# Expert products of a mixture layer: all 1024 gate columns first, then the up columns, instead of two half-width passes over both

## What is computed

```python
gu = rows @ w_gate_up[e] + b_gate_up[e]          # 1024 -> 2048
gate = jnp.minimum(gu[:, :D_FF], SWIGLU_LIMIT)   # D_FF = 1024, limit 7
up = jnp.clip(gu[:, D_FF:], -SWIGLU_LIMIT, SWIGLU_LIMIT)
hid = (up + 1.0) * (gate * jax.nn.sigmoid(gate * SWIGLU_ALPHA))
return hid @ w_down[e] + b_down[e]               # 1024 -> 1024
```

## Time and profile before

| | us |
|---|---|
| median of 3 runs | 2472.63 (2472.3 to 2474.09) |
| the profiled execution, its own time | 2471.6 |
| its span, first to last instruction | 2469.9 |
| PE busy | 2341.7 |
| DVE busy | 1807.0 |
| ACT busy | 1402.9 |
| granted TensorE clock, mean | 0.979 of full speed |

### The profile page before, as it was taken

How to read it: one execution, slowest core, us unless ns; L and a number is a source line. 1 busy time by engine, 2 the same in 40 slices (tenths; PEclk the granted TensorE clock), 3 DMA queues, 4 the chain that set the end, 5 groups by cost and what they waited for, 6 DMA issues and landing times.

```text
span 2469.9 us, 39207 instructions
## 1 busy us (share of the span) xinstructions
PE 2341.7 (95%) x11242; PEld 1577.9 (64%) x11243; DVE 1807.0 (73%) x2101; ACT 1402.9 (57%) x1441; POOL 257.3 (10%) x252
## 2 busy tenths in 40 slices
PE   6999999999948999999999999999999999999898
PEld 3454445545536777677777777777776777776443
DVE  4582555544557889788989988898877787897374
ACT  2112354434435777667777777677766676776344
POOL 1200000001230000100000001000111010010230
PEclk9999999999959999999999999999999999999999
DMA  6006910052238999999999999899988898997761
GB/s 198 22 13 216 355 36 22 14 185 77 69 96 287 333 352 354 336 311 362 345 375 351 360 365 348 307 338 375 351 287 312 278 360 292 367 347 260 267 221 51
DMA packets 291338, 629.50 MB, mean 255 GB/s; under 512 B 21633, under 2 KB 69505, under 8 KB 291218
## 3 DMA queue, kind: packets, MB, share of 16 engines
q1 hardware_dynamic: 235538, 532.20, 61.4%
q10 hardware_dynamic: 40304, 55.05, 6.2%
q0 software_dynamic: 15440, 41.51, 5.2%
HBM read 558.55 MB, written 68.57 MB: 254 GB/s over the span
## 4 chain that ended last, share of the span: by engine, by line
PE 75%; DVE 12%; issue 5%; DMA 5%; ACT 2%; DVEq 1%; SPq 1%; POOL 0%; ACTq 0%; POOLq 0%
PE bank L610 13%; PE bank L612 12%; PE bank L611 12%; PE bank L1368 6%; DVE wlo L876 6%; PE bank L780 4%; PE bank L1481 4%; PE bank L1391 3%; PE bank L671 3%; DMA raw<-in_w_down_dram 3%; PE bank L1358 2%; PE bank L1411 2%; PE bank L1440 2%; PE bank L1426 2%; PE bank L580 2%
## 5 line engine op out<-in xcount | busy, mean ns | idle before, releaser
L876 DVE TENSOR_TENSOR wlo<-raw,whi 128x2048 fp32r<-128x2048 f32 x456 | 1038.1, 2287 | 203.2 <-PE bank L612 159.8
L1753 ACT ACTIVATE whi<-raw 128x2048 fp32r<-128x2048 f32 x456 | 872.4, 1915 | 351.0 <-PE bank L612 172.8
L610 PE MATMUL bank<-whi,xhi 128*128 128x512 f32 x1216 | 498.3, 410 | 4.2 <-issue 4.2
L612 PE MATMUL bank<-wlo,xhi 128*128 128x512 f32 x1216 | 481.4, 396 | 0.0
L611 PE MATMUL bank<-whi,xlo 128*128 128x512 f32 x1216 | 481.0, 396 | 0.0
L610 PEld LDWEIGHTS bank<-whi,xhi 128*128 128x128 f32 x1216 | 228.7, 188 | 93.3 <-issue 43.4
L612 PEld LDWEIGHTS bank<-wlo,xhi 128*128 128x128 f32 x1216 | 228.8, 188 | 55.0
L611 PEld LDWEIGHTS bank<-whi,xlo 128*128 128x128 f32 x1216 | 229.1, 188 | 47.0
L610 PE MATMUL bank<-whi,hhi 128*128 128x512 f32 x608 | 246.0, 405 | 0.0
L612 PE MATMUL bank<-wlo,hhi 128*128 128x512 f32 x608 | 237.6, 391 | 0.0
L611 PE MATMUL bank<-whi,hlo 128*128 128x512 f32 x608 | 236.9, 390 | 0.0
(11 more groups left out here) (294 smaller groups left out, 2767.3 us busy)
## 6 DMA issues: line engine op xcount, KB each, us to landing
raw<-in_w_gate_up_dram SPq DMA_DIRECT2D x608, 512.0 KB, 6.5
raw<-in_w_down_dram SPq DMA_DIRECT2D x152, 1024.0 KB, 10.5
expert_rows<-zeros ACTq DMA_DIRECT2D x1, 33280.0 KB, 105.5
expert_rows<-ysb ACTq DMA_DIRECT2D x38, 512.0 KB, 8.1
xall<-in_x_dram SPq DMA_DIRECT2D x8, 512.0 KB, 11.0
uT<-in_w_out_dram SPq DMA_DIRECT2D x1, 4096.0 KB, 12.8
raw<-in_w_ple_gate_dram SPq DMA_DIRECT2D x1, 4096.0 KB, 19.8
h<-h_scratch SPq DMA_DIRECT2D x8, 512.0 KB, 6.2
```

The lines of the kernel that those rows point to most:

```text
L610: pe.matmul(dst, stat_hi[:, kt], hi, start=first, stop=False)
L612: return pe.matmul(dst, stat_hi[:, kt], lo, start=False, stop=last)
L876: dve.tensor_tensor(wlo[:, c % LO], raw[:, c % RAW], whi[:, c % HI].bitcast(F32), ALU.subtract).then_inc(lo_ready, 1)
L1753: act.activation(whi[:, c % HI], raw[:, c % RAW], ACT.Copy).then_inc(hi_ready, 1)
```

## The change

Pieces 0 to 3 now hold 256 rows of all 1024 gate columns, pieces 4 to 7 those of the up columns; each is one transfer with rows of 4 KB. Gate is limited once, 1024 wide, after piece 3; one sigmoid and one product of that width follow. On ACT the sigmoid stands behind hi of piece 9, as the first half's did. On DVE the product now stands before lo of piece 8. PE computes the first half (512 columns) of pieces 6 and 7, signals `up_done`, and then does their second halves; the first transposition of `hid` stands between these two. The next item's rows are transposed after piece 7 instead of after piece 8. DVE's lo of pieces 9, 10, 11 and 0', 1', 2' is moved one step later in its program. The tail has one chain of width 256 for gate and one for up: limit of gate after piece 3', transposes after piece 4.

```diff
-                half, p = c // 4, c % 4
-                rows = w_gate_up[0, bass.ds(e, 1), p * 256:p * 256 + 256, :].rearrange(
+                g, p = c // 4, c % 4
+                rows = w_gate_up[0, bass.ds(e, 1), p * 256:p * 256 + 256, g * DFF:g * DFF + DFF].rearrange(
                     "e (k p) n -> p (e k) n", p=P)
-                for g in range(2):
-                    sp.dma_start(parts[:, g], rows[:, :, g * DFF + half * 512:g * DFF + half * 512 + 512]
-                                 ).then_inc(raw_in[slot], 16)
+                sp.dma_start(dst.rearrange("p (k d) n -> p k (d n)", k=2), rows).then_inc(raw_in[slot], 16)
...
             def gate_piece(n, c, turns):
+                if c == 6:
+                    gate_part(n, 6, 0)
+                    pe.wait_ge(lo_ready, PIECES * n + 8)
+                    gate_part(n, 7, 0).then_inc(up_done, 1)
+                if c == 7:
+                    turns()
+                if c < 6:
+                    gate_part(n, c, 0)
+                return gate_part(n, c, 1)
...
+            def gate_clamp(n):
+                dve.wait_ge(w_free, PIECES * n + 4)
+                dve.wait_ge(hid_ready, 2 * n)
+                dve.wait_ge(gs_done, n)
+                dve.tensor_scalar(gat[:], banks(gate_base(0), 2), LIMIT, None, ALU.min).then_inc(gat_ready, 1)
+            def gate_product(n):
+                dve.wait_ge(sig_done, n + 1)
+                dve.tensor_tensor(sig[:], gat[:], sig[:], ALU.mult).then_inc(gs_done, 1)
+            def up_half(n, half):
+                if half == 0:
+                    dve.wait_ge(up_done, n + 1)
+                else:
+                    dve.wait_ge(w_free, PIECES * n + 8)
...
+                dve.tensor_scalar(upc[:], banks(gate_base(1) + half), LIMIT, -LIMIT, ALU.min, ALU.max).then_inc(gu_used, 1)
+                dve.wait_ge(gs_done, n + 1)
...
                 dve.scalar_tensor_tensor(out=hid[:], in0=upc[:], scalar=1.0, in1=sig[:, half * 512:half * 512 + 512], ...)
...
             def body(n, k1, tail):            # DVE
                 for c in range(PIECES):
+                    if c == 3:
+                        gate_clamp(n)
+                    if tail and c == 4:
+                        tail_up(k1)
+                        tail_gated(k1)
+                    if c == 4:
+                        gate_product(n)
                     if c == 5:
                         items.ahead(n + 1)
+                    if c in (6, 7):
+                        up_half(n, c - 6)
...
+                    if c < 5:
                         dve.wait_ge(w_free, PIECES * n + c + 1)
                         split_lo(n, c + LO)
+                    if c in (6, 7, 8):
+                        dve.wait_ge(w_free, PIECES * n + c)
+                        split_lo(n, c + LO - 1)
+                    if c == 6:
+                        hidden(n, 0)
+                    if c >= 9:
                         with dve.If(nxt > 0):
                             if c == 9:
                                 columns(n + 1)
+                            dve.wait_ge(w_free, PIECES * n + c)
+                            split_lo(n + 1, c + LO - PIECES - 1)
+                            if c == 11:
+                                dve.wait_ge(w_free, PIECES * n + PIECES)
+                                split_lo(n + 1, LO - 1)
...
             def body(n, k1, tail):            # PE
-                    if tail and c == 1:
-                        turn_tail_hidden(k1, 0)
+                    if tail and c == 4:
+                        turn_tail_hidden(k1)
-                    if c == 8:
+                    if c == 7:
...
                         with pe.If(nxt > 0):
                             turn_rows(n + 1)
...
             def body(n, k1, tail):            # ACT
+                    if tail and c == 5:
+                        tail_hidden(k1)
+                    elif c == 7:
...
+                            split_hi(n + 1, c + HI - PIECES)
+                            columns(n + 1)
...
                     if c == 3:
-                        sigmoid(n, 0)
+                        sigmoid(n)
```

More of the change, by code:

```diff
@@ L510, in raw_value @@
         def raw_value(n, c):
[L512 to L514 removed]
+            return 32 * n + 16 * (c // RAW + 1)
         class Items:
@@ new lines, in gate_part @@
+            def gate_part(n, c, half):
+                g, p = c // 4, c % 4
+                base = gate_base(g)
+                if p == 0 and half == 0:
+                    if g == 0:
+                        pe.wait_ge(xlo_ready, n + 1)
+                        pe.wait_ge(y_used[0], n)
+                    else:
+                        pe.wait_ge(gu_used, 2 * n)
+                if p == 0 and half == 1:
+                    if g == 0:
+                        pe.wait_ge(bias_in[0], 32 * n + 32)
+                        pe.wait_ge(y_used[1], n)
+                    mm = bias_pair(base, g, True)
+                    if g == 1:
+                        mm.then_inc(bias_used[0], 1)
+                for k in range(2):
+                    mm = three(banks(base + half), xhi, xlo, 2 * p + k, c, 2 * k + half,
+                               p == 0 and half == 0 and k == 0, p == 3 and k == 1)
+                return mm
@@ L682, in tail_piece, with turn_tail_hidden @@
                 mm.then_inc(tail_free, 1)
[L684 to L687, removed]
+            def turn_tail_hidden(k1):
+                hold(pe, hid_t_ready, k1 + 1)
+                hold(pe, ht_ready, k1)
+                for s in range(2):
+                    mm = pe.transpose(banks(XT)[:, s * P:s * P + P], hid_t[:, s * P:s * P + P], ident)
+                mm.then_inc(htt_done, 1)
             turn_rows(0)
@@ L976, in body @@
                                 columns(n + 1)
[L977 to L984, removed]
+                            dve.wait_ge(w_free, PIECES * n + c)
[3 more added lines that the diff above has]
+                                split_lo(n + 1, LO - 1)
                     if c == 11:
                         with dve.If(nxt2 > 0):
-                            tail_first(nk1, 0, items.kf + tail)
+                            tail_gate(nk1, items.kf + tail)
             items.run(body)
@@ L1821, in body @@
                         act.activation(mark[:], ident[:, 0:1], ACT.Sigmoid).then_inc(table_set, 1)
-                    if c == 7:
-                        sigmoid(n, 1)
-                    if tail and c == 5:
-                        tail_sigmoid(k1, 1)
                     if c in (6, 8):
                         hidden(n, c // 8)
-                    if tail and c == 6:
-                        tail_hidden(k1, 1)
+                    if c == 6:
+                        with act.If(nxt2 > 0):
+                            tail_columns(nk1)
                     if c == 11:
```

178 lines of the change are left out of this document (70 added, 108 removed).

## The result

The changed kernel takes 2510.42 us (median; 2508.51 to 2510.92, 4 runs) where the kernel before, on the same chip, takes 2472.47: a ratio of 1.0151, 95% interval 1.0139 to 1.0163. Forecast were 2504 us, so +32 against a measured +38. The direction and most of the size came out; the place did not. The forecast had over two thirds of the loss in plain items. Nearly all of it sits in the six items that stand before a tail, and in the tail items.

What follows compares the result with a forecast made beforehand. PE's 38.0 us per item and the nearly equal ring of raw slots were taken as the bound. Plain items +22.8, before tails +9, behind tails +1.5, tail items -1.6 made +32: 2504 us, own range 2484 to 2525, overall 2456 to 2535.

Steps and rivals of the forecast that it cites:

- The chain: DVE and ACT, plain item: first up limit follows hi of 9, sigmoid, product, lo of 8, register reads; 0.5 us late.
- register reads 1.08: DVE, plain item: register reads between lo of piece 8 and the first up limit take 1.08 us.
- U: Start of the first up limit on DVE: 1.5 us late in every plain item, with nothing hiding it.
- Piece 9 in plain items: Load of piece 9 lands 1.0 us later than today, between bounds of 0 and 2.5.
- The ring of slots: Raw slots for pieces 5' and 6' come free 3.1 and 3.6 us later, as DVE's lo's move back.
- PE alone: PE's own work in a plain item: changes sum to -0.32 us, so an item could take 37.7.
- Items before a tail: Six plain items before a tail: its traffic comes 4 us earlier and meets piece 9; net +1.5 us each.
- The upper bound of 2.5: Most by which piece 9 lands later: slots 3.1 us later, less 3 x 0.2 for shorter transfers.
- Tail items: Eight items with a tail: PE waits 0.4 us less in piece 1, 0.25 more in piece 7; -0.2 each.
- Items behind a tail: Five plain items after a tail: the longer tail item has filled the ring; +0.3 us each.
- the ring is not late: Rival: piece 9 lands at least 0.5 us sooner, plain items gain 0.3, kernel 2456 us; chance 0.22.
- 2 us less for a piece in one transfer: DMA estimate from the skill's page: standing alone, a piece costs 4.4 us in one transfer, 6.4 in two.

Runs made afterwards that it cites:

- ScalarE's order: Changed kernel with ScalarE applying the sigmoid before it makes the bf-rounded part of piece 9, not behind it: 2467.12 us, ratio 0.9987.
- VectorE's order: Changed kernel with VectorE making the lo of piece 8 before the gate's product, the sigmoid left in place: 2481.89 us, ratio 1.0046.
- the cured kernels: Changed kernel with sigmoid ahead of piece 9's rounding (2467.12 us), lo of piece 8 ahead of the product (2481.89), or sigmoid and TensorE's reads moved ahead (2456.52).
- both cures: Changed kernel with the sigmoid ahead of piece 9's rounding and TensorE's register reads ahead of the hold for hid_t: 2456.52 us, ratio 0.9942.
- the later broadcasts: Changed kernel with GpSimd's eight tail bias broadcasts held until a semaphore TensorE raises behind piece 4: 2497.05 us, ratio 1.0101.
- GpSimd's requests later: Changed kernel with GpSimd's next row requests held for a semaphore TensorE raises behind piece 8's transpose: 2511.99 us, ratio 1.0175.

## Why the prediction was right, and where it was wrong

**The chain, right, with one false term.** That the first `up` limit would stand behind hi of 9, sigmoid, product and lo of 8 is what the traces show, and two cures at different links of it (ScalarE's order, VectorE's order) remove the wait in plain items. The step that failed is "register reads 1.08". Before, they followed `hid`, 0.69 long, and showed as idle time; now they follow a lo of 2.28 us and no idle time shows, so they run beside it. With 1.08 less, a landing as before would leave the chain 0.6 us early and not 0.5 late; with the landing 1.0 later as forecast, U is 0.4 late and not 1.5. In the item shown it is 0.5 late: the last matmul of both first halves starts at 1251.33, plus 0.52 makes 1251.85, and the limit starts at 1252.38. That is why plain items gained 0.1 instead of 1.2 us: 22.8 us of the sum were 1.9.

**Piece 9 in plain items, right**: 1.0 us later was taken from bounds of 0 and 2.5, and 0.96 was measured. The ring of slots is the cause that the trace bears out, though no run changed it alone: SP issues the loads of pieces 5' and 6' 3.1 and 3.4 us later against the item's start than before (means of the plain items; forecast 3.1 and 3.6), and that of piece 9 2.6 later. That 1.0 of the 2.6 is left at the landing was a choice between the bounds. PE alone was put at 37.7; the cured kernels do an item in 37.5 to 37.7.

**Items before a tail, mechanism right, size wrong.** The tail's traffic does come earlier and meets piece 9: 3.3 us by the broadcasts' mean start (9.6 to 6.3), near the forecast's 4. But the delay was taken as up to 2.5 us with +1.5 net per item, 9 us in all; it was 4.3 us and +5.5 per item, 32.8 us. Two things were missed. The upper bound of 2.5 was worked out for the ring alone, and the tail's delay comes on top. And a wait of about 4 us was priced at itself, while the clock behind it costs some 3 us more. The Trainium skill, TensorE: Matmul & The Clock Gate, section "HAM oscillation — how this bites in real kernels", tells of matmul kernels whose wait for data throttles the engine so that the next tile starts cold; the traces here agree, with 0.50 granted behind all six waits of 3.8 to 4.6 us, and show it behind several shorter ones too. It was not weighed in the prediction.

**Tail items, wrong sign.** The forecast was -0.2 each, from the tail's wait that goes, and that wait did go. It missed that the one hold now stands directly ahead of PE's register reads, which before had matmuls in front: +1.46 each, 10.2 us, taken back by moving three lines. **Items behind a tail**: +0.3 forecast, -0.4 measured.

That +32 came out near +38 is luck, for 24 us too little before tails and 12 too little in tail items met 21 too much in plain items, 3 too much behind tails and the 5 that item 0 gained. **The rival "the ring is not late"** (2456) needed piece 9 sooner; it was later. What it said of the value of a chain without a wait is what both cures give, 2457, with the piece as late as ever: its price was right for another cause. The estimate that the prediction worked out from the Trainium skill, DMA: Bandwidth & Descriptors, section on the anatomy of one DMA, 2 us less for a piece in one transfer, does not show here: undoing it moved piece 9 by 0.6 us. The section's figure is for transfers that GpSimd issues, and these are SyncE's.

## What to carry to other kernels

When the consumers of an operation move, list anew what it stands behind in its in-order queue, and ask of each whether it waits for a transfer. Here a sigmoid of 1.04 us kept its place behind piece 9's rounding, where the kernel before had it too; once what PE needs next hung on it, through a product, a lo and a limit, that place cost 43 us with its input ready. Price a new long wait of the matmul engine with the clock behind it, not alone (here some 3 us on top of waits near 4 us), and look first at the items in which several delays meet. Put register reads ahead of a hold, or where a long operation is queued in front of them.

## What the runs showed of the hardware that I had not expected

The clock falls behind waits of very different lengths. Behind the plain items' waits of 1.20 to 1.42 us in the changed kernel, and of up to 1.67 with the later broadcasts, it stayed at 1.00. In an item before a tail, with the sigmoid first, it fell to 0.50 for 3.4 us behind one of 1.09 us, and matmuls step by 0.43 us:

```profile
1001.61 0.66 PE L591 MATMUL bank<-cst,hid 128*128 128x128 f32 x4 [1.09 <-DVE hid L911]
...
1003.85 0.63 PE L604 MATMUL bank<-whi,xhi 128*128 128x512 f32 x1
1004.28 0.63 PE L605 MATMUL bank<-whi,xlo 128*128 128x512 f32 x1
```

Waits of 1.41 us (kernel before), 2.27 us (lo first) and 3.36 us (above) left it at 1.00. A fall lasted from 3 to 11 us behind the wait. What beside the wait decides is open. In items before a tail the transposes of the tail's rows (L582) stand right behind the wait, as they do not in plain ones; no run moved them alone.

A semaphore that TensorE's sequencer raises by itself comes ahead of matmuls that stand before it in the program: 2.1 us before the last of them had signalled in the run with GpSimd's requests later (973.43 and 975.55), 4.4 us in the run with the broadcasts later (996.89 and 1001.33). One that is attached to a matmul comes with it: DVE starts 0.52 us after that matmul's start.
